# Sharing one square between two triangles of scores in a sliding-window attention

## The reference, cut to what matters

```python
def swa_attention(q, k, v, sinks):
    ...
    s = jnp.einsum('bnqhgd,bnkhd->bnhgqk', qb, kw) * scale
    diff = t_loc + BLOCK - j_loc
    mask = (diff >= 0)[None] & (diff < SWA_WINDOW)[None] & (key_abs >= 0)
    s = jnp.where(mask[None, :, None, None], s, NEG_INF)
    m = jnp.maximum(jnp.max(s, axis=-1, keepdims=True), sink)
    e = jnp.exp(s - m)
    denom = jnp.sum(e, axis=-1, keepdims=True) + jnp.exp(sink - m)
    p = (e / denom).astype(v.dtype)
    o = jnp.einsum('bnhgqk,bnkhd->bnqhgd', p, vw)
```

## Time and profile before

| what | value |
| --- | --- |
| median of three runs | 2195.8 us (2195.43 to 2196.14) |
| profiled execution, its time | 2195.6 us |
| profiled execution, its span | 2193.4 us |
| TensorE busy | 2176.6 us, 99% of the span |
| VectorE busy | 1610.6 us, 73% |
| ScalarE busy | 1315.8 us, 60% |
| chain that ended last | TensorE 97%, VectorE 2% |
| mean granted TensorE clock | 0.999 |

### The profile page before, as it was taken

One profiled execution on the slowest core, in us unless ns is written; L12 is line 12 of the kernel. 1 busy time (PEld: TensorE's weight loads), 2 busy tenths in 40 slices (PEclk: granted clock), 3 DMA queues, 4 the chain that ended last, 5 costly groups with the idle time before them and its releaser, 6 DMA issues.

```text
span 2193.4 us, 34379 instructions
## 1 busy us (share of the span) xinstructions
PE 2176.6 (99%) x13434; PEld 1882.4 (86%) x13434; DVE 1610.6 (73%) x2921; ACT 1315.8 (60%) x2491; POOL 9.7 (0%) x22
## 2 busy tenths in 40 slices
PE   8999999999999999999999999999999999999998
PEld 8888888888898888888888888888888888888887
DVE  7797655687688887755777867777677767698864
ACT  6766345775476666544666655555556655566754
POOL 0000000000000000000000000000000000000000
PEclk9999999999999999999999999999999999999999
DMA  7543333566455555555555555555555455544464
GB/s 269 173 142 119 117 125 132 182 225 201 163 173 192 189 187 191 188 190 190 191 185 190 192 183 192 183 182 184 191 178 171 166 196 184 190 155 146 140 208 142
DMA packets 107329, 389.29 MB, mean 177 GB/s; under 512 B 12272, under 2 KB 12272, under 8 KB 106400
## 3 DMA queue, kind: packets, MB, share of 16 engines
q1 hardware_dynamic: 104976, 377.31, 50.6%
q0 software_dynamic: 1904, 9.47, 1.2%
q10 hardware_dynamic: 288, 0.32, 0.0%
HBM read 384.34 MB, written 2.13 MB: 176 GB/s over the span
## 4 chain that ended last, share of the span: by engine, by line
PE 97%; DVE 2%; ACT 0%; issue 0%; DMA 0%; DVEq 0%; SPq 0%; ACTq 0%
PE main L495 89%; PE two L495 7%; PE two L498 1%; DVE WL L914 0%; DVE gt L914 0%; DMA RAW<-ws 0%; DVE GQ L920 0%; PE main L541 0%; ACT PP L1547 0%; DVE PP L920 0%; DVE FQ L914 0%; DVE PP L914 0%; ACT WH L1547 0%; ACT FQ L1547 0%; ACT L1546 0%
## 5 line engine op out<-in xcount | busy, mean ns | idle before, releaser
L1547 ACT ACTIVATE WH<-RAW 128x512 fp32r<-128x512 f32 x1416 | 884.1, 629 | 681.9 <-PE main L495 674.3
L914 DVE TENSOR_TENSOR WL<-RAW,WH 128x512 fp32r<-128x512 f32 x1416 | 962.6, 688 | 400.8 <-ACT WH L1547 391.8
L495 PE MATMUL main<-A,WH 128*128 128x512 f32 (+1 forms) x3680 | 1146.9, 394 | 8.0 <-DVE WL L914 7.9
L495 PEld LDWEIGHTS main<-A,WL 128*128 128x128 f32 x3584 | 674.7, 188 | 154.6
L495 PE MATMUL main<-A,WL 128*128 128x256 f32 x3584 | 715.2, 279 | 0.0
L495 PEld LDWEIGHTS main<-A,WH 128*128 128x128 f32 x3680 | 564.0, 190 | 22.2 <-issue 10.9
L495 PE MATMUL main<-H,WH 128*128 128x512 f32 x704 | 221.2, 395 | 0.0
L495 PE MATMUL main<-B,WH 128*128 128x512 f32 (+1 forms) x640 | 184.4, 374 | 0.0
L495 PEld LDWEIGHTS main<-H,WL 128*128 128x128 f32 x704 | 132.3, 188 | 31.2
L495 PE MATMUL main<-H,WL 128*128 128x256 f32 x704 | 138.5, 278 | 0.0
L495 PE MATMUL main<-WH,A 128*128 128x512 f32 (+1 forms) x448 | 137.7, 382 | 0.0
(11 more groups left out here) (295 smaller groups left out, 1704.4 us busy)
## 6 DMA issues: line engine op xcount, KB each, us to landing
RAW<-ws SPq DMA_DIRECT2D x708, 512.0 KB, 3.3
CB<-cscr POOLq DMA_DIRECT2D x4, 1024.0 KB, 4.8
xs<-xT SPq DMA_DIRECT2D x8, 256.0 KB, 7.5
XT<-xT POOLq DMA_DIRECT2D x4, 512.0 KB, 7.7
MS<-memT POOLq DMA_DIRECT2D x4, 512.0 KB, 7.7
out<-YT SPq DMA_DIRECT2D x7, 256.0 KB, 2.6
CST<-cst SPq DMA_DIRECT2D x1, 1248.0 KB, 7.1
G<-g POOLq DMA_DIRECT2D x1, 1024.0 KB, 6.6
```

Of the source, the lines that this page charges most:

```text
L495: return e.matmul(o, l, r, start=start, stop=True, skip_group_check=True)
L914: return e.tensor_tensor(o, a, b, op)
L1547: return e.activation(o, i, f, bias=bias, scale=scale, accum_out=accum)
```

## The change

Queries 128 to 255 keep one square of 128 columns per head instead of two. After masking, VectorE takes the maximum of both triangles' squares (a masked place holds -1e30), and maxima, exponentials, sums and products go over 256 columns of a head instead of 384. `turn` transposes two squares per head instead of three. The turned square is then taken apart by VectorE: times `tri` (1 where the key's place is at or before the query's) gives the turned lower triangle, and the square minus that gives the other. ScalarE copies only the first square, at tick 17 instead of 16, and both it and the weighing wait for VectorE. VectorE's generator has a fourth signal per block (`W_VE` = 4). The two masking passes are one instruction of 768 columns.

```diff
@@ -438,6 +438,7 @@
         Q_PE, Q_VE, Q_AC, Q_MU = 21, 29, 11, 8
         S_PE, S_VE, S_AC = 3, 3, 2
         F_PE, F_VE, F_AC = 3, 3, 2
+        W_VE = 4
 
 
         def sync_program(e):
@@ -831,9 +832,9 @@
                 mm(b[:, 0:128], qa[:, 0:128], ka[:, 0:128])
                 return mm(b[:, 128:384], qa[:, 128:256], ka, start=False)
 
-            def turn(S, two):
+            def turn(S, two, blocks=3):
                 for h in range(2):
-                    for j in range(3):
+                    for j in range(blocks):
                         z = tr(two[h][:, 128 * j:128 * j + 128], S[:, h, 128 * j:128 * j + 128])
                 return z
 
@@ -873,7 +874,7 @@
 
                     w.wait_ge(y_done, 16 + m - 3)
                 if m >= 2:
-                    w.wait_ge(wp_ve[(m - 2) % SWA_LANES], F_VE * ((m - 2) // SWA_LANES) + 1)
+                    w.wait_ge(wp_ve[(m - 2) % SWA_LANES], W_VE * ((m - 2) // SWA_LANES) + 1)
                 for h in range(2):
                     P = slice(64 * h, 64 * h + 64)
                     z = scores(AQ[P, 4 * g + p, :], KR[P, g, :], two[h])
@@ -881,10 +882,11 @@
                 yield from ticks(15)
                 if m < 14:
 
-                    w.wait_ge(wp_ve[(m + 2) % SWA_LANES], F_VE * ((m + 2) // SWA_LANES) + 1)
-                w.wait_ge(wp_ve[lane], F_VE * i + 3)
-                turn(PPw[lane], two).then_inc(wp_pe[lane], 1)
+                    w.wait_ge(wp_ve[(m + 2) % SWA_LANES], W_VE * ((m + 2) // SWA_LANES) + 1)
+                w.wait_ge(wp_ve[lane], W_VE * i + 3)
+                turn(PPw[lane], two, 2).then_inc(wp_pe[lane], 1)
                 yield from ticks(3)
+                w.wait_ge(wp_ve[lane], W_VE * i + 4)
                 w.wait_ge(wp_ac[lane], 2 * i + 2)
                 cols = [slice(64 * g, 64 * g + 64)] * 2
                 weigh(two[0], WV, cols, PTw[m % 2]).then_inc(wp_pe[lane], 1)
@@ -1401,12 +1403,12 @@
                 w.wait_ge(lf_pe, 2)
                 e.tensor_copy(SM[:, 128:192], banks[6][:, 0:64]).then_inc(lf_ve, 1)
 
-            def soft(S, mx, dn, done_sem, lag, exp_sem, exp_n, masked, sink=None, sk=None):
+            def soft(S, mx, dn, done_sem, lag, exp_sem, exp_n, masked, sink=None, sk=None, end=384):
 
                 yield from ticks(2 * lag)
                 w.wait_ge(done_sem, masked)
                 e.tensor_reduce(mx[:, 0:2], S[:, :, 0:128], AX, ALU.max)
-                z = e.tensor_reduce(mx[:, 2:4], S[:, :, 128:384], AX, ALU.max)
+                z = e.tensor_reduce(mx[:, 2:4], S[:, :, 128:end], AX, ALU.max)
                 if sink is not None:
                     h2 = lambda a: a.rearrange("p (a b) -> p a b", a=2)
                     w.wait_ge(v_own, own(z))
@@ -1423,7 +1425,7 @@
                 z = e.reciprocal(dn, dn)
                 w.wait_ge(v_own, own(z))
                 tt(S[:, :, 0:128], S[:, :, 0:128], bc(dn[:, 0:2], 128), ALU.mult)
-                tt(S[:, :, 128:384], S[:, :, 128:384], bc(dn[:, 2:4], 256), ALU.mult).then_inc(done_sem, 1)
+                tt(S[:, :, 128:end], S[:, :, 128:end], bc(dn[:, 2:4], end - 128), ALU.mult).then_inc(done_sem, 1)
 
             def fox(g, p):
                 lane, i = p % 2, 2 * g + p // 2
@@ -1446,14 +1448,26 @@
             def swa(g, p):
                 m = 4 * g + p
                 lane, i = m % SWA_LANES, m // SWA_LANES
-                S, bank = PPw[lane], banks[5 + 2 * (m % 2)]
+                S, two = PPw[lane], twos[m % 2]
                 mx, dn, sk = (SM[:, 8 + 24 * lane + 4 * k:12 + 24 * lane + 4 * k] for k in range(3))
                 yield from ticks(1 + m % 2)
                 w.wait_ge(wp_pe[lane], F_PE * i + 1)
-                tt(S[:, 0, :], banks[4 + 2 * (m % 2)][:, 0:384], band, ALU.min)
-                tt(S[:, 1, :], bank[:, 0:384], band, ALU.min).then_inc(wp_ve[lane], 1)
+                z = tt(S[:], two[:, :, 0:384], bm(band, 2), ALU.min)
+                z.then_inc(wp_ve[lane], 1)
+
+
+                w.wait_ge(wp_ve[lane], W_VE * i + 1)
+                t = own(tt(S[:, :, 128:256], S[:, :, 128:256], S[:, :, 256:384], ALU.max))
                 sink = PAR[:, P_SINK + 8 * g + 2 * p:P_SINK + 8 * g + 2 * p + 2]
-                yield from soft(S, mx, dn, wp_ve[lane], 2, wp_ac[lane], 2 * i + 1, F_VE * i + 1, sink, sk)
+                w.wait_ge(v_own, t)
+                yield from soft(S, mx, dn, wp_ve[lane], 2, wp_ac[lane], 2 * i + 1, W_VE * i + 1, sink, sk, 256)
+                yield from ticks(7 - m % 2)
+
+                w.wait_ge(wp_pe[lane], F_PE * i + 2)
+                P, sq = PTw[m % 2], two[:, :, 128:256]
+                t = own(tt(P[:, :, 256:384], sq, bm(K["tri"], 2), ALU.mult))
+                w.wait_ge(v_own, t)
+                tt(P[:, :, 128:256], sq, P[:, :, 256:384], ALU.subtract).then_inc(wp_ve[lane], 1)
 
             def gate(g, late):
                 kind, gt = ("w", GTS[g]) if late else ("f", GTF[g])
@@ -1822,8 +1836,8 @@
                 w.wait_ge(lf_pe, 3)
                 copy(CTN[0:32, :], banks[7][0:32, 0:256], scale=-1.0).then_inc(lf_ac, 1)
 
-            def exps(S, mx, dn):
-                for j, (x0, x1) in enumerate(((0, 128), (128, 384))):
+            def exps(S, mx, dn, end=384):
+                for j, (x0, x1) in enumerate(((0, 128), (128, end))):
                     for h in range(2):
                         n = 2 * j + h
                         z = act(S[:, h, x0:x1], S[:, h, x0:x1], ACTF.Exp, bias=mx[:, n:n + 1], accum=dn[:, n:n + 1])
@@ -1849,13 +1863,14 @@
                 S, bank = PPw[lane], banks[4 + 2 * (m % 2)]
                 mx, dn, sk = (SM[:, 8 + 24 * lane + 4 * k:12 + 24 * lane + 4 * k] for k in range(3))
                 yield from ticks(6 + m % 2)
-                w.wait_ge(wp_ve[lane], F_VE * i + 2)
-                exps(S, mx, dn)
+                w.wait_ge(wp_ve[lane], W_VE * i + 2)
+                exps(S, mx, dn, 256)
                 act(sk, sk, ACTF.Exp).then_inc(wp_ac[lane], 1)
-                yield from ticks(10 - m % 2)
-                w.wait_ge(wp_pe[lane], F_PE * i + 2)
-                copy(PTw[m % 2][:], twos[m % 2][:, :, 0:384]).then_inc(wp_ac[lane], 1)
-                yield from ticks(3)
+                yield from ticks(11 - m % 2)
+
+                w.wait_ge(wp_ve[lane], W_VE * i + 4)
+                copy(PTw[m % 2][:, :, 0:128], twos[m % 2][:, :, 0:128]).then_inc(wp_ac[lane], 1)
+                yield from ticks(2)
                 w.wait_ge(wp_pe[lane], F_PE * i + 3)
                 if m == 12:
                     w.wait_ge(rp_done, len(ROPED))
```

## The result

| | median | runs |
| --- | --- | --- |
| before | 2195.69 us | 6 |
| changed | 2202.88 us (2202.59 to 2203.26) | 6 |

The ratio is 1.0033 with a 95% interval of 1.0022 to 1.0044: the change makes the kernel 7.2 us slower. The forecast was 4.9 us slower (2200.6 against 2195.7). The profiled execution has a span of 2201.1 us, 7.7 more than the one before.

A forecast was written before the change was run, and what follows sets the result against it. TensorE was taken to bound the kernel, busy 40.00 of 40.00 us in the second layer's attention, VectorE close behind. Waits of 8.1 us against 3.3 us saved gave +4.8 us, a median of 2200.6 us, range 2198 to 2204.

The forecast's parts named there:

- place of the passes after the transposes: On VectorE: when it reaches the new passes after a pair's first transpose; 4.2, 5.2, 4.5, 3.8 us in pairs 1, 2, 3, 8.
- fifth to seventh pair: At the weighing: no wait, since passes end by 4.1 us and the copy by 4.5, under TensorE's arrival at 5.19.
- waits for the copy of the result: On ScalarE: a late copy of the turned square pushes the copy of the result, 0.3 us in two or three pairs.
- What it takes away: On TensorE: 32 transposes go at 0.1025 us each, saving 3.3 us; four fewer bring the weighing forward to 5.19 us.
- what VectorE pays: On VectorE: narrower softmax pays for the merging, net nothing; taking the square apart adds 1.58 us a pair, 12.6 in all.
- The new wait: Before the weighing: TensorE waits for VectorE's passes and ScalarE's copy, 7.8 us summed over pairs one to four and eight.
- The rival of the clock: On TensorE: half rate behind the eighth pair's 3.3 us stop loses 2.1 us more, giving 2202.7 us; chance 0.06.
- The cover holds: Between turning and weighing: the new passes and copy fit into 5.19 us, only transposes count, 2192.5 us; chance 0.15.
- only the eighth pair waits: At the weighing: ScalarE's order, not VectorE's load, causes the wait; -3.3 + 3.4 gives 2195.9 us; chance 0.10.
- VectorE becomes the bound: On VectorE: low halves arrive late too, all 12.6 us show plus 1.7 for the eighth pair, 2206.8 us; chance 0.09.
- One sign did not come: In the new profile: VectorE was to be busy above 38 of 40 us around 1980.

The follow-up runs named there:

- the kernel with the eighth pair mended: Changed kernel with ScalarE's copy of the turned square put back to tick 16 in the eighth pair alone: 2198.17 us, +2.3 against before.
- the load-only kernel: Changed kernel with VectorE's two passes on scores nobody reads, ScalarE copying all 768 columns at tick 16, weighing waiting only for that copy: 2196.39 us.

## Why the prediction was right in kind and short in size

The numbers in order, for pairs 1, 2, 3, 4 and 8. The waits are the delays of the weighing against the 5.15 us of the pairs that do not wait, from first transpose to first weighing matmul; the changed kernel's are 5.93, 6.57, 6.84, 6.72 and 9.06.

| term | predicted | measured |
| --- | --- | --- |
| transposes | -3.3 | -3.6 on the way to the weighing; -3.1 net, with transposes alone left out |
| VectorE's passes, a pair | 1.58 | 1.58 |
| place of the passes after the transposes, pairs 1, 2, 3, 8 | 4.2, 5.2, 4.5, 3.8 | 4.3, 5.1, 4.6, 4.2 |
| waits at the weighing | 0.6, 1.3, 1.3, 1.3, 3.3 | 0.8, 1.4, 1.7, 1.6, 3.9 |
| fifth to seventh pair | none | none |
| waits for the copy of the result | 0.3 | none in the list of waits, about 0.1 by the distances to the scores |
| clock after the eighth pair's stop | a rival, 2.1 | 1.3 in the weighing, 0.3 after it |

- *What it takes away* held, and so did *what VectorE pays*: the 768-column pass takes 0.95 us, and between transposes and weighing the passes stand where the walk through VectorE's order put them, to 0.1 us in the first three pairs. The transposes are worth a little more than was read: twelve take 1.23 us, but eight take 0.79 (1949.19 to 1949.98 in the changed kernel), so the four that go are worth 0.44 and not 0.41.
- *The new wait* held in mechanism, and its size was off: 7.8 predicted, 9.4 measured. The copy ends 0.15 us before the weighing's first matmul starts, five times; the sums ended at the end of the copy. That is 0.7 of the 1.6. In the eighth pair I had let narrower products bring the place forward by 0.5 us. It came at 4.24, as before the change (4.28), and the wait grew by 0.4. VectorE is in step with ScalarE at two points there: a high half released it 0.2 us later after the seventh weighing than before the change, and its wait for a gate grew from 0.34 to 0.60 us:

```profile
2074.05 0.42 DVE L916 TENSOR_TENSOR Y<-Y,GT 128x256 f32<-128x256 f32 x1 [0.60 <-ACT GT L1561]
```

Together that is the half microsecond that the products had saved. The third and fourth pair were put at 1.3, inside their bounds of 0.6 and 1.6, and came at the upper one: ScalarE's exponentials, released late, counted in full, as the third pair's rows show.
- *The rival of the clock* is no rival but came on top of the forecast. It had a chance of 0.06 as a case by itself; its trigger, a stop of more than 3 us, was already in the forecast, so it should have been added to it: with 1.6 us more the forecast had been 2202.2.
- *The cover holds* fell with five of eight pairs; *only the eighth pair waits* fell with pairs one to four, and the kernel with the eighth pair mended, still at +2.3, shows it a second time. *VectorE becomes the bound* was wrong as put (the low halves are never late in the changed kernel), though the load-only kernel shows that VectorE's added time costs without any new wait at the weighing, by way of ScalarE and the scores.
- *One sign did not come.* VectorE was to be busy above 38 of 40 us around 1980. It was busy 37.14, little more than the 36.87 before, while TensorE, at 37.02, stood still for the rest:

```profile
1960.00:2000.00 40.00, 37.02 (x246) 31.34 (x244) 37.14 (x89) 22.48 (x68) 0.00 (x0) 1.00 0.41 137
```

  So a share of busy time near that of before does not show that an engine has room for more work.

Adding up: -3.6 + 9.4 + 1.6 + 0.1 = +7.5. The stage also began 0.15 us later in this execution (first scores at 1924.71, before at 1924.56), which makes 7.65 against a span 7.7 longer. The runs' medians differ by 7.2; between one profiled execution and the medians such half microseconds stay open.

## What to carry to other kernels

An instruction moved off the busiest engine is paid for by the engine it lands on, and the price is not its duration but how late that engine then reaches the things others wait for: here 12.6 us of VectorE work bought 3.1 us of TensorE's, on an engine with 3.1 us of rest in 40, and cost 10.3. Before adding a step to a chain between two engines, walk the receiving engine's list in order from the last idle gap and compare the place with the moment of need; and if the step is linear, look for an operand that can be changed once instead of a result that has to be changed each time. Where a long stop is forecast on TensorE, add what the clock costs behind it, here 1.6 us behind a stop of 3.84 us and 1.65 us behind one of 2.0.

## What the runs showed of the hardware

- TensorE's clock fell after a stop of 3.84 us in the midst of 2200 us of work: 16 matmul records took 2.79 us from their start to the next row instead of 1.50, and the granted clock was 0.59, then 0.56, before it was 1.00 again in the window from 2094. In the kernel with the copy at tick 16 everywhere, whose longest wait in this stage was 2.0 us, the windows behind that stop (2095 to 2100) read

```profile
2095.00:2100.00 5.00, 5.00 (x24) 4.02 (x21) 4.75 (x12) 4.23 (x10) 0.00 (x0) 0.69 0.38 120
```

  and with 1.6 us as the stage's longest wait (the eighth pair mended) the clock stayed at 1.00. By the Trainium skill (TensorE: Matmul & The Clock Gate, What's actually happening) the rate is halved once the array has been idle and released again by activity; the trace agrees, with the fall seen behind a stop as short as 2.0 us here, which may hang on what went before it.
- ScalarE hands over to TensorE more slowly than VectorE to ScalarE: 0.15 us from the end of the copy to the first matmul (1974.77 to 1974.92; that matmul's weight load begins at 1974.88, 0.11 us after the copy), and 0.04 us from the end of a pass to the start of the copy (1974.35 to 1974.39).
